# Weighing of two heads in column halves, with repeated softmax inverses turned as one block

## The reference, cut

```python
# mixer A: 8 heads of 64, own chunk of 64 tokens and 8 chunks before it, learned bias
sc = jnp.einsum('bqhd,bkhd->bhqk', qc, kc) * scale + bias
p = jax.nn.softmax(sc, axis=-1)
o = jnp.einsum('bhqk,bkhd->bqhd', p, vc)
# mixer B: 8 query heads, 2 key heads, own chunk and the one before, rotary q and k, a sink per head
m = jnp.maximum(jnp.max(sc, axis=-1, keepdims=True), sink)
p = jnp.exp(sc - m)
p = p / (jnp.sum(p, axis=-1, keepdims=True) + jnp.exp(sink - m))
o = jnp.einsum('bnhgqk,bnkhd->bnqhgd', p, vb)
```

## Time and profile before

| | |
|---|---|
| median of 3 runs | 2675.07 us (2673.93 to 2676.16) |
| the profiled execution | 2678.14 us, span 2676.2 us |
| TensorE busy | 2631.9 us, 98% of the span |
| VectorE busy | 1923.2 us, 72% |
| ScalarE busy | 1159.0 us, 43% |
| GpSimd busy | 252.6 us, 9% |
| attention, layer 1 | 281.76 to 519.30 us of the span |
| attention, layer 2 | 1605.80 to 1840.30 us of the span |

### The profile page before, as it was taken

How to read it: one execution, slowest core, us unless ns; L and a number is a source line. 1 busy time by engine, 2 the same in 40 slices (tenths; PEclk the granted TensorE clock), 3 DMA queues, 4 the chain that set the end, 5 groups by cost and what they waited for, 6 DMA issues and landing times. The chain is left out here.

```text
span 2676.2 us, 36725 instructions
## 1 busy us (share of the span) xinstructions
PE 2631.9 (98%) x12920; PEld 2208.2 (83%) x12920; DVE 1923.2 (72%) x3579; ACT 1159.0 (43%) x2429; POOL 252.6 (9%) x390
## 2 busy tenths in 40 slices
PE   8999999999999999999999999999999999999998
PEld 6888888888888888888878888888888888888886
DVE  8766667644787787767996666775448887776687
ACT  6222677732533333344542227775325333333444
POOL 0000311244100000000000011112440000000000
PEclk9999999999999999999999999999999999999999
DMA  4323433253222332385423243332531332234843
GB/s 147 122 104 115 155 102 111 75 183 115 87 99 103 114 118 84 106 269 176 153 99 122 99 144 123 119 97 88 188 120 61 114 110 88 103 114 136 267 124 126
DMA packets 185236, 333.21 MB, mean 125 GB/s; under 512 B 17248, under 2 KB 62688, under 8 KB 185056
## 3 DMA queue, kind: packets, MB, share of 16 engines
q1 hardware_dynamic: 176832, 307.67, 34.6%
q10 hardware_dynamic: 8224, 23.20, 2.6%
HBM read 237.09 MB, written 92.80 MB: 123 GB/s over the span
## 5 line engine op out<-in xcount | busy, mean ns | idle before, releaser
L1203 PE MATMUL ps<-op_hi,up_hi 128*128 128x512 f32 x1232 | 479.9, 390 | 2.5 <-DVE third_sum L2781 2.5
L1205 PE MATMUL ps<-op_hi,up_lo 128*128 128x512 f32 x1232 | 479.3, 389 | 0.0
L1204 PE MATMUL ps<-op_lo,up_hi 128*128 128x512 f32 x1232 | 479.3, 389 | 0.0
L1203 PE MATMUL ps<-in_hi,up_hi 128*128 128x512 f32 x728 | 286.9, 394 | 3.3 <-DVE up_lo L2279 2.1
L1205 PE MATMUL ps<-in_hi,up_lo 128*128 128x512 f32 x728 | 285.0, 392 | 0.0
L1204 PE MATMUL ps<-in_lo,up_hi 128*128 128x512 f32 x728 | 285.0, 392 | 0.0
L1878 ACT ACTIVATE up_hi<-up_raw 128x512 fp32r<-128x512 f32 x252 | 158.0, 630 | 276.9 <-PE ps L1205 271.1
L1203 PEld LDWEIGHTS ps<-op_hi,up_hi 128*128 128x128 f32 x1232 | 231.3, 188 | 51.1 <-issue 3.3
L1205 PEld LDWEIGHTS ps<-op_hi,up_lo 128*128 128x128 f32 x1232 | 231.3, 188 | 48.3
L1204 PEld LDWEIGHTS ps<-op_lo,up_hi 128*128 128x128 f32 x1232 | 231.3, 188 | 47.6
L1173 POOL CAST w_hi<-w_raw 128x256 fp32r<-128x256 f32 x192 | 85.3, 486 | 1757.7 <-DMA w_raw<-w_lin 1199.7
(11 more groups left out here) (266 smaller groups left out, 5406.8 us busy)
## 6 DMA issues: line engine op xcount, KB each, us to landing
up_raw<-w_gu SPq DMA_DIRECT2D x42, 1024.0 KB, 5.1
act_raw<-ff_saved SPq DMA_DIRECT2D x154, 256.0 KB, 2.7
w_quarter<-w_lin SPq DMA_DIRECT2D x52, 512.0 KB, 4.4
w_raw<-w_lin SPq DMA_DIRECT2D x48, 512.0 KB, 3.7
ff_saved<-ff_block SPq DMA_DIRECT2D x88, 256.0 KB, 2.0
ff_saved<-ff_mix SPq DMA_DIRECT2D x66, 256.0 KB, 2.1
gated<-gates_saved SPq DMA_DIRECT2D x32, 512.0 KB, 4.1
stage<-in_saved SPq DMA_DIRECT2D x48, 256.0 KB, 2.8
```

The source lines that it names most:

```text
L1203: pe.matmul(out, w1, x1, start=first, stop=False, skip_group_check=True)
L1204: pe.matmul(out, w1, x0, start=False, stop=False, skip_group_check=True)
L1205: return pe.matmul(out, w0, x1, start=False, stop=last, skip_group_check=True)
```

## The change

Weighing is done for both heads of a pair in one place, on even steps. The stationary operand is now a block of values, 64 columns for each head, and the moving one the turned probabilities, 128 columns. Head 0 writes partitions 0 to 63 of PSUM and head 1 partitions 64 to 127, and the matmuls of the two heads alternate. The result has features on the partitions, as `x_sb` wants it, so the pair itself isn't turned any more. Instead the inverses, which vary along the free dimension there, are made as a block: `invert_pair` writes each of the two inverses of a token 64 times (`wide`, 128 x 128), TensorE turns it (`turn_wide`), ScalarE copies it into the place of the result in `x_sb` (`take_wide`), and `take_heads` multiplies the weighed pair from PSUM into it.

With it go: a third place for turned probabilities (`probs_t`, `NTURNED`), in B one place for both heads of a pair, whose probabilities are turned together and copied by one instruction of 256 columns; in B two places in each `probs` buffer (`soft`, `soft_last`); `take_heads` behind row_max instead of ahead of it; `FILL_A` with its gate steps in other places, of the same number; one logit buffer (the last one excepted), so that `scale_logit` waits for the store of the logit before; `vb_odd` in two parts, with three DMAs for the first half of the values instead of two; `head_done` counted in pairs; attention loops that end two steps earlier; and `split_o`, which waits for `head_free`.

```diff
-FILL_A = ((3, 3, 3, 2, 2, 2, 2, 1, 1, 1, 1, 1, 1, 1, 1, 1), (1, 1, 1, 1, 1, 0, 1, 0, 1, 0, 0, 0, 1, 0, 0, 0))
+FILL_A = ((3, 3, 3, 3, 2, 3, 1, 2, 1, 1, 0, 1, 1, 1, 0, 1), (0, 1, 0, 2, 0, 1, 0, 1, 0, 1, 0, 1, 0, 1, 0, 0))
...
+def groups_turned(u):
+
+    g, r = divmod(u + 1, UNITS_PER_GROUP)
+    return g * (PHASE + PHASE // 2) + min(r, PHASE) + max(r - PHASE, 0) // 2
+
+
+TURN_GROUPS = GROUPS * (PHASE + PHASE // 2)
+HEAD_PAIRS = UNITS // 2
...
-        probs_t = [at(f"probs_t{i}", [P, A_COLS], F32, 101 * KB + 2560 * i) for i in range(2)]
+        probs_t = [at(f"probs_t{i}", [P, A_COLS], F32, (101 * KB, 103 * KB + 512, TAB + 5 * KB + 512)[i]) for i in range(NTURNED)]
         stat = at("stat", [P, NSTAT, 8], F32, 63 * KB + 512)
-        o_tok = at("o_tok", [P, 2, P], F32, TAB + 14592)
+        wide = at("wide", [P, 2, P], F32, TAB + 14592)
...
+        w_ps = bank(7)[:, 2 * P:3 * P]
+
+        def x_of(u):
+
+            mixer, g, _, p = unit(u)
+            if mixer == "A":
+                return x_sb[:, g, p * P:(p + 1) * P]
+            tile, chunk = GROUPS + g // 2 * 2, chunk_of(g, p)
+            return x_sb[:, tile:tile + 2, chunk * CHUNK:(chunk + 1) * CHUNK]
+
+        def turned_to(u):
+
+            mixer, _, _, _ = unit(u)
+            return probs_t[u % NTURNED if mixer == "A" else u // 2 % 2]
...
+        def logit_of(i):
+            return logit[1 if i == GATE_HALVES - 1 else 0][:, :]
...
-                if u > 0:
-                    pe.wait_ge(turned_ready, L * UNITS + u)
+                if u > 0 and (mixer == "A" or e == 0):
+                    pe.wait_ge(turned_ready, L * TURN_GROUPS + groups_turned(u - 1))
+                first = e if mixer == "B" else 0
                 for j in range(key_blocks(mixer, p)):
-                    mm = pe.transpose(t_ps[:, j * P:(j + 1) * P], probs[u % NPROBS][:, j * P:(j + 1) * P], ident[:, :])
+                    mm = pe.transpose(t_ps[:, (first + j) * P:(first + j + 1) * P], soft(u)[:, j * P:(j + 1) * P], ident[:, :])
                 mm.then_inc(turned, 1)
 
             def weigh(L, u):
 
-                mixer, g, e, p = unit(u)
+                mixer, g, _, p = unit(u)
                 nb = key_blocks(mixer, p)
+                n = L * HEAD_PAIRS + u // 2
                 if mixer == "A":
-                    values = [va[:, p + 1 - nb + j, e * HD:(e + 1) * HD] for j in range(nb)]
-                    if e == 0 and p % 2 == 0:
+                    blocks = [va[:, p + 1 - nb + j, :] for j in range(nb)]
+                    turns = [turned_to(u - 1), turned_to(u)]
+                    if p % 2 == 0:
                         pe.wait_ge(v_ready, L * VALUES + V_PARTS * rank(CONV.index(("va", g, p // 4))) + p % 4 // 2 + 1)
                 else:
                     chunk = chunk_of(g, p)
-                    v, block = (vb, chunk // 2) if chunk % 2 or chunk == 0 else (vb_odd, chunk // 2 - 1)
-                    values = [v[:, block, e * HD:(e + 1) * HD]]
-                    if e == 0 and p == 0:
+                    blocks = [vb[:, chunk // 2, :] if chunk % 2 or chunk == 0 else odd_values(chunk // 2 - 1)]
+                    turns = [turned_to(u)[:, e * P:(e + 1) * P] for e in range(2)]
+                    if p == 0:
                         pe.wait_ge(v_ready, L * VALUES + V_PARTS * (rank(CONV.index(("vb", 0, min(g, 1)))) + 1))
-                    if e == 0 and (g, p) in ((0, 2), (1, 0)):
-                        pe.wait_ge(vb_shifted[g], 32 * (L + 1))
-                pe.wait_ge(turned_ready, L * UNITS + u + 1)
-                n = L * (UNITS // 2) + u // 2
+                    if (g, p) in ((0, 2), (1, 0)):
+                        pe.wait_ge(vb_shifted[g], (48, 32)[g] * (L + 1))
+                pe.wait_ge(turned_ready, L * TURN_GROUPS + groups_turned(u))
                 taken = n - 1 if mixer == "B" and u % PHASE > 1 else n
-                if e == 0 and taken > 0:
+                if taken > 0:
                     pe.wait_ge(head_free, taken)
                 for j in range(nb):
-                    mm = pe.matmul(o_ps(u)[:, e * HD:(e + 1) * HD], probs_t[u % 2][:, j * P:(j + 1) * P], values[j],
-                                   start=(j == 0), stop=(j == nb - 1))
+                    for e in range(2):
+                        rows = slice(e * HD, (e + 1) * HD)
+                        mm = pe.matmul(o_ps(u)[rows, :], blocks[j][:, rows], turns[e][:, j * P:(j + 1) * P],
+                                       start=(j == 0), stop=(j == nb - 1))
                 mm.then_inc(head_done, 1)
 
-            def turn_pair(L, u):
-
-                n = L * (UNITS // 2) + u // 2
-                pe.wait_ge(head_free, n + 1)
+            def turn_wide(L, s, u):
+
+                n = L * HEAD_PAIRS + u // 2
+                pe.wait_ge(inverse_ready, n + 1)
                 if n > 0:
-                    pe.wait_ge(pair_ready, n)
-                pe.transpose(p_ps, o_tok[:, n % 2, :], ident[:, :]).then_inc(pair_turned, 1)
+                    pe.wait_ge(wide_ready, n)
+                if values_before(s) > 0:
+                    pe.wait_ge(v_ready, L * VALUES + values_before(s))
+                pe.transpose(w_ps, wide[:, n % 2, :], ident[:, :]).then_inc(wide_turned, 1)
...
-                for s in range(UNITS + 5):
+                for s in range(UNITS + 3):
                     if s < UNITS:
                         scores(L, s)
                     steps = fill_steps(s)
                     for i, k in steps[:1]:
                         gate_step(L, i, k)
-                    if 2 <= s < UNITS + 2:
-                        turn(L, s - 2)
-                    if 3 <= s < UNITS + 3:
+                    u = s - 2
+                    if 0 <= u < UNITS:
+                        if unit(u)[0] == "A":
+                            turn(L, u)
+                        elif u % 2:
+                            turn(L, u - 1)
+                            turn(L, u)
+                    if s >= 4 and s % 2 == 0:
+                        turn_wide(L, s, s - 3)
                         weigh(L, s - 3)
                     for i, k in steps[1:]:
                         gate_step(L, i, k)
-                    if s > 5 and s % 2 == 0:
-                        if values_before(s) > 0:
-                            pe.wait_ge(v_ready, L * VALUES + values_before(s))
-                        turn_pair(L, s - 5)
                     for c, part in turns_at(s):
-                        if s > 6:
-                            pe.wait_ge(pair_ready, L * (UNITS // 2) + (s - 5) // 2)
+                        if s > 3:
+                            pe.wait_ge(wide_ready, L * HEAD_PAIRS + (s - 2) // 2)
                         turn_values(L, c, part)
...
             def take_turned(L, u):
                 mixer, _, _, p = unit(u)
-                cols = key_blocks(mixer, p) * P
+                cols = key_blocks(mixer, p) * P if mixer == "A" else 2 * P
...
+                act.activation(turned_to(u)[:, 0:cols], t_ps[:, 0:cols], ACT.Copy).then_inc(turned_ready, 1)
...
-                if mixer == "A":
-                    act.activation(x_sb[:, g, p * P:(p + 1) * P], p_ps, ACT.Copy).then_inc(pair_ready, 1)
-                else:
-                    tile, chunk = GROUPS + g // 2 * 2, chunk_of(g, p)
-                    act.activation(x_sb[:, tile:tile + 2, chunk * CHUNK:(chunk + 1) * CHUNK],
-                                   p_ps.rearrange("p (h n) -> p h n", h=2), ACT.Copy).then_inc(pair_ready, 1)
+                mixer, _, _, _ = unit(u)
+                act.wait_ge(wide_turned, L * HEAD_PAIRS + u // 2 + 1)
+                src = w_ps if mixer == "A" else w_ps.rearrange("p (h n) -> p h n", h=2)
+                act.activation(x_of(u), src, ACT.Copy).then_inc(wide_ready, 1)
...
-                dve.reciprocal(st[:, :, 6:7], total).then_inc(inverse_ready, 1)
+                n = L * HEAD_PAIRS + u // 2
+                if n >= 2:
+                    dve.wait_ge(wide_turned, n - 1)
+                dve.reciprocal(wide[:, n % 2, :].rearrange("p (e d) -> p e d", e=2), total.to_broadcast([P, 2, HD])).then_inc(inverse_ready, 1)
 
             def take_heads(L, u):
 
-                n = L * (UNITS // 2) + u // 2
-                dve.wait_ge(head_done, L * UNITS + u + 1)
-                dve.wait_ge(inverse_ready, n + 1)
-                if u >= 4:
-                    dve.wait_ge(pair_turned, n - 1)
-                inverse = stat[:, u % NSTAT - 1:u % NSTAT + 1, 6:7].to_broadcast([P, 2, HD])
-                dve.tensor_tensor(o_tok[:, n % 2, :].rearrange("p (e d) -> p e d", e=2),
-                                  o_ps(u).rearrange("p (e d) -> p e d", e=2), inverse, ALU.mult).then_inc(head_free, 1)
+                mixer, _, _, _ = unit(u)
+                n = L * HEAD_PAIRS + u // 2
+                dve.wait_ge(head_done, n + 1)
+                dve.wait_ge(wide_ready, n + 1)
+                src = o_ps(u) if mixer == "A" else o_ps(u).rearrange("p (h n) -> p h n", h=2)
```

(21 more changed lines are left out.)

68 lines of the change are left out of this document (42 added, 26 removed).

## The result

The changed kernel takes **2704.83 us** (median of 4 runs, 2700.09 to 2705.53), the kernel before 2674.5 in the same series: ratio 1.0111, 95% interval 1.0093 to 1.0128. The forecast was 2645, 30 us faster; the kernel is 30 us slower. It lies 60 us above the forecast and 19 above the upper end of the range, 2686. The profiled execution has 2705.05 us (span 2703.1).

The account below looks back on a forecast made before the run. TensorE was taken as the bound. Terms -64.5 (weighing), +13.4 (uneven step), +9, +8.5, +4.4 and +1 (VectorE), -2 (tail) sum to -30 us, from the median of 2675.07 to 2645; range 2618 to 2686.

Parts of the forecast that it names:

- Weighing, -64.5: Weighing on TensorE: two passes, one of each head, stand in the time of one, a gain of 64.5 us.
- a rival, with a chance of 0.17: TensorE's array empties at each change between whole and halved columns: 41 us, 20 at the end, 2665 us; chance 0.17.
- turn_wide, 0: turn_wide on TensorE, ahead of the weighing, waits for the reciprocal of two steps before: 0 us.
- Reciprocal and VectorE, +23: Reciprocal of 128 columns takes 0.87 us; VectorE's queue costs +9 in A1 to A3, +8.5 B1/B2, +4.4 B0, +1 elsewhere.
- the growing slope: Sign for VectorE as bound: the reciprocal's time per column, 5.3 to 6.5 ns in the trace, grows with size.
- its rival: VectorE becomes the bound, row_max waiting behind a reciprocal of 1.2 us: 2682 us; chance 0.13.
- not over 90: Sign of being right: VectorE over 90% busy in B1, the second B stretch of attention.
- The uneven step, +13.4: Weighing both heads on even steps leaves odd steps waiting in the score loop, in A stretches: 13.4 us lost.
- ScalarE: 0: ScalarE's copies: 64 fewer in B, a third place for turned probabilities unties A, busy time falls: 0 us.
- Logit buffer, 0: scale_logit waiting for the store of the logit before: 0 us, or +1 to +3 if SP is late in A0.
- Tail, -2: End of each layer's attention: two steps fewer, ending on the weighing, 2 us gained over both layers.
- a fall inside attention: Sign of being wrong: the granted clock falls inside attention, where it showed 1.00 before.

Follow-up runs that it names:

- e4: The changed kernel with the weighing ordered head by head, all blocks of head 0 and then all of head 1: 2732.42 us.
- e3: The changed kernel with one full-width weighing matmul for each block instead of two half-width ones (not a correct result): 2684.53 us.
- e1: The changed kernel with turn_wide issued behind the weighing and the gate steps instead of ahead of them: 2687.72 us.
- e5: The kernel before with an extra, unused reciprocal of 104 columns in front of the one of 2: 2695.18 us against 2673.59.
- e7: The changed kernel with turn_wide behind the gate steps, and a reciprocal of 2 columns plus an ordinary copy repeating it 64 times: 2680.83 us.
- e11: e7 with turn_wide directly behind the scores in even steps that don't follow a turning of values: 2680.98 us.
- e6: The changed kernel with the edits of e1 and e3 together (not a correct result): 2674.24 us, ratio 1.0003 to the kernel before.
- e9: e7 with the change undone in mixer B alone, mixer A keeping the column halves: 2680.31 us.

## Why the prediction was wrong

Two views bear on the first step. A pair of B before, its two heads and the transpose:

```profile
391.25 0.33 PE L1373 MATMUL ps<-vb_odd,probs_t 128*128 128x64 f32 x2
391.39 0.31 PE L1337 MATMUL ps<-kb_hi,qb_first 128*128 128x128 f32 x1
...
392.49 0.33 PE L1373 MATMUL ps<-vb_odd,probs_t 128*128 128x64 f32 x2
392.66 0.28 PE L1383 MATMUL ps<-ident,o_tok 128*128 128x128 f32 x1
392.70 0.30 PE L1337 MATMUL ps<-kb_hi,qb_second 128*128 128x128 f32 x1
```

And one after:

```profile
396.83 0.27 PE L1436 MATMUL ps<-ident,wide 128*128 128x128 f32 x1
397.03 0.44 PE L1424 MATMUL ps<-probs_t,vb_odd 128*64 128x128 f32 x4
397.40 0.33 PE L1384 MATMUL ps<-kb_hi,qb_second 128*128 128x128 f32 x1
```

By its own steps:

- **Weighing, -64.5.** The overlap is real (e4) and the pace of two passes in 0.11 us right. Two things failed. The step set the change of mode at nothing and gave it to a rival, with a chance of 0.17; the rival's 41 us raw and 20 at the end were 38 and 20 (e3). And it carried 0.106 us a pass from pairs of five blocks to the 72 pairs of one. In B a head's two passes took 0.14 to 0.17 us and a finished pair's transpose 0.04, so 0.35 a pair; now weighing and turn_wide are 0.37 + 0.20. So a one-block pair loses 0.22. By the same reading one of two blocks gains about 0.03, of three 0.25, of four 0.50, of five (1.05 + 1.05 + 0.04 for 1.24 + 0.20) 0.70. Over 72, 8, 8, 8 and 32 pairs that is 15.8 - 6.2 - 22.4 = **-13** in place of -64.5, an estimate from these paces. This is the largest error, some 52 us of TensorE time.
- **turn_wide, 0.** It named the wait for the reciprocal and not the one for the values, which the diff moved ahead of the weighing with it. The reciprocal's wait was 2.8 us, the values' 19. e1: **17 us** (with some of the clock's 2.7 in it).
- **Reciprocal and VectorE, +23.** 951 ns were measured for 870, within the range given; 104 columns took 800, so 6.2 to 6.3 ns a column. The 21.6 us of e5 are the forecast's size, but by luck: they come in the old order, mostly by another wait. In the changed kernel's order 68 of the 100 us of work were worth 7 (e7). The prediction also took "the growing slope" as a sign for its rival; its own three sizes have 6.5 and then 5.25 ns a column, which doesn't grow. The Trainium skill's repeat count of 8 for Reciprocal ("VectorE: DVE Perf Modes"), which gave an estimate of 1.2 us, does not fit as 8.3 ns a column; the measurement decides. VectorE is 84% busy in A1 and 85% in B1, not over 90: what it costs comes from the order in its queue, since it never was full.
- **The uneven step, +13.4.** The odd step with a gate step was right: 1.90 forecast, 1.91 measured. The even one was taken as 2.37 and is up to 3.08: 0.18 more in the weighing and 0.09 in turn_wide from the mode, 0.05 in the scores, and 0.37 because the turn waits for the one place of turned probabilities, a loop that the step did not look at, under "ScalarE: 0". e11 shows that filling this wait alone gains nothing. (The third place for turned probabilities is in SBUF; the one in PSUM stayed single.)
- **Logit buffer, 0**: right. scale_logit idles 0.2 us in all 32. **Tail, -2**: right; from the first scores of B3 to the first gate product on `o_hi` it takes 36.5 us for 37.8 and, in layer 2, for 37.7.
- **The clock.** The prediction named a fall inside attention as a sign of being wrong. It came once, behind the longest of the new waits, and cost 2.7 us.

So the step that failed first is the weighing term: -64.5 us, with the change of mode at nothing and a pace from pairs of five blocks carried to those of one. The runs showed about -13, and 20 us at the end for the mode alone (e3). The second is turn_wide's 0, which was 17 (e1).

The sum does not close to the microsecond by single edits, since waits stand in for one another: e1 and e3 alone give 17 and 20, together 30.6. With both, the kernel is back at the time of the one before (e6). The reciprocal's share is smaller in the new order, 7 us beside the moved `turn_wide` (e7). What stays open is the share of each remaining wait in the last 7 us that e7, e9 and e11 have over the kernel before. Nor was the single PSUM place for turned probabilities doubled in any run, or the new place of `take_heads` tried by itself.

## What to carry to other kernels

Price a halved column mode by the visit, not by the pass: here 0.3 us to go in and out, while each further block of float32 work saves some 0.23, so that one block loses 0.22 us, two break even and five gain 0.70. When an instruction is moved ahead of another, move its waits with it on paper, and ask for each what the other now waits for. What an engine's extra work costs in one order of its queue says little about another order: the reciprocal cost 21.6 us in the old one (e5) and shortening it gained 7 in the new one (e7). A pace read in a long run of passes does not hold for a run of one or two.
